# Scan heads: the second group of score matmuls issued directly behind the first, ahead of the value rows' first tile

## The chip, the cores and the metric

One Trainium2 chip, one of its eight cores. The metric is the device time of one execution in microseconds (us). The figure of a kernel is the median of its runs, and lower is better.

## The reference: what is computed

One step of a two-layer decoder trunk over 512 prompt tokens and 8 sequences of 8 new tokens (576 columns in all), with D = 1024. Each layer is an adaLN-modulated norm, an input projection, a mixer, a gate and an output projection with a gated residual. Layer 0 mixes with HGRN2, a gated linear recurrence with 8 heads (128 key features, 256 value features), and layer 1 with dilated window attention. The change lies in layer 0 only, in the part that makes each head's score matrix:

```python
q = silu(q);  f = lb + (1 - lb) * sigmoid(f + b_f);  k = 1 - f
b = cumsum(log f)                        # within a chunk
A[t, s] = sum_c q[t, c] k[s, c] exp(b[t, c] - b[s, c])    # s <= t
o = A v + (q exp(b)) S                   # S: state carried over chunks
```

## The kernel before

Five engines run programs of their own in a fixed order written by hand, and semaphores join them. TensorE (PE) is the engine that all others serve.

**Matmuls.** A projection is done in three passes of rounded fp32 operands (`w_hi`·`h_hi`, `w_hi`·`h_lo`, `w_low`·`h_hi`). ScalarE (ACT, L412) and VectorE (DVE, L419) split each weight piece into its two parts, and PE waits for `raw_split`.

**The scan of layer 0.** `pe_step(pe, h)` runs for h = 0 to 9. Step h projects the inputs of head h and scans head g = h - 1, whose keys and queries were made one step earlier. From h = 1 to 7 both are done, so what is told of a "step" below happens seven times. In order, PE does in such a step:

1. the queries of head h (`project_T`, L446), then a mean for head h - 2, then the gates of head h (L446);
2. the scores of head g, in three groups. The decay between two positions is taken level by level (1, 2, 4, ... 64 positions), and each level is a set of small matmuls with 32-column weights and 32 columns of data. `pe_grams(pe, g, 0)` does levels 0 to 2 (60 matmuls, PSUM bank `X[:, 0]`), `pe_grams(pe, g, 1)` levels 3 to 5 (20 + 16 + 16 = 52 matmuls, bank `X[:, 1]`, L1293), and group 2 the two widest levels (L1299, bank `X[:, 2]`);
3. the value rows of head h (`project_rows`, L467), four tiles of 128 tokens with 24 matmuls of 256 columns each. `project_rows` calls `between(tile)` behind each tile, and `between` puts other work there: behind tile 1 a transpose of adaLN rows (L525), score group 2 and a part of the second layer's adaLN projection (L493);
4. behind tile 3 the transposes of the scanned head's keys (`pe_turn_keys`, L1309 and L1319), which also wait for `ada_done`, that is for DVE's reading of the adaLN rows (`read_ada_chunk`, L565 and L557); in steps 1 to 6 two more adaLN projections (L493); then the sequences' rows (L1335, L1339), the chunk states (L1352), which wait for ACT's `kr` (L1013) and DVE's `kz` (L1167), and the rest. In step 7 the adaLN projections are absent, behind tile 1 as well as behind tile 3.

Meanwhile DVE reads score group 0 (L1069, L1073), makes the running sum `b_` (L1180), reads score group 1 (L1073 again), and then works through the levels of head h (L1103, L1104, L935, L936), with group 2 (L1083 to L1089), the adaLN rows and `kz` among them.

In the trace each of these score matmuls leaves two records, so that 60 are 120 records and 52 are 104.

Of the kernel before, what the change touches and what calls it, by code (L numbers as in the profile page):

```python
# [128 lines left out]
def program(nc, I, O):  # L129
    with ExitStack() as ctx:  # L130
# [133 lines left out]
        def ticket_w(h, t):  # L264
            return TICKETS * h + t
# [134 lines left out]
        def parts_of(key):  # L400
            nk, width = stream[index[key]][2:4]
            return [w[:, 0:nk * width].rearrange("p (k c) -> p k c", k=nk) for w in (hi_buffer(key), lo_buffer(key))]
# [23 lines left out]
        def begin(t):  # L426
            if t >= 2:
                wait_read(nc.tensor, t - 2)
            return t % 2
# [7 lines left out]
        def project_T(t, key, ks=range(KD), cut=HT):  # L437

            nc.tensor.wait_ge(raw_split, split_no[key][0] + 1)
            s = begin(t) if 0 in ks else t % 2  # L440
            wh, wl = parts_of(key)
            for k in ks:
                for i, (a, b) in enumerate(((wh, h_hi), (wh, h_lo), (wl, h_hi))):
                    for e in range(2):
                        n0, n1 = (0, cut) if e == 0 else (cut, T)
                        last = nc.tensor.matmul(PJ[:, 2 * s + e, 0:n1 - n0], a[:, k, :], b[:, k, n0:n1],  # L446
                                                start=(k == 0 and i == 0), stop=(k == KD - 1 and i == 2))
            if KD - 1 in ks:
                last.then_inc(pj_ready, 1)

        def row_passes(tile, k, wh, wl):

            rows = slice(tile * P, tile * P + P)
            if tile == CH:
                return ((h_hi[:, k, rows], wh), (h_hi[:, k, rows], wl))
            return ((h_hi[:, k, rows], wh), (h_lo[:, k, rows], wh), (h_hi[:, k, rows], wl))

        def project_rows(t, keys, tiles, out_of, between=None):

            begin(t)  # L460
            for tile in tiles:
                for k in range(KD):
                    if k % 4 == 0:
                        nc.tensor.wait_ge(raw_split, split_no[keys[k // 4]][0] + 1)
                    passes = row_passes(tile, k, *parts_of(keys[k // 4]))
                    for i, (a, b) in enumerate(passes):
                        last = nc.tensor.matmul(out_of(tile), a, b[:, k % 4, :], start=(k == 0 and i == 0),  # L467
                                                stop=(k == KD - 1 and i == len(passes) - 1))
                if tile == tiles[-1]:
                    last.then_inc(pj_ready, 1)  # L470
                if between:
                    between(tile)
# [830 lines left out]
        def pe_turn_keys(pe, g):  # L1303

            pe.wait_ge(lv_done, XS * g + XS)
            if g:
                pe.wait_ge(fin_done, 2 * g)
            for c in range(CH):
                pe.transpose(X[:, 3, c * P:(c + 1) * P], kh[:, c * P:(c + 1) * P], ident[:])  # L1309
            pe_turn_seq_keys(pe, g)  # L1310
# [44 lines left out]
        def pe_seq_out(pe, g):  # L1355

            pe.wait_ge(orow_done, g + 1)
            for j in range(2):
                last = pe.transpose(X[:, 2, 256 + j * P:256 + (j + 1) * P], orow[:, j * P:(j + 1) * P], ident[:])
            last.then_inc(os_ready, 1)  # L1360
# [9 lines left out]
        def pe_mean(pe, f):  # L1370

            halved = f < AH - 2
            if halved:
                pe.wait_ge(sum_done, f + 1)
            else:
                pe.wait_ge(sq_done, f + 1)
            pe.wait_ge(ub_read, f + 1)
            for bank, a, z in ((0, 0, TP), (1, TP, T)):
                for j in range(1 if halved else 2):
                    last = pe.matmul(X[:, bank, 0:z - a], ones[:], sq0[:, j, a:z], start=(j == 0), stop=(halved or j == 1))  # L1380
            last.then_inc(ms_ready, 1)

        def pe_step(pe, h):
            b, g, f = h % 2, h - 1, h - 2
            new, scan, end = h < AH, 0 <= g < AH, 0 <= f
            if new and h:
                project_T(ticket_w(h, 0), ("w", h, 0))
            if end and new:
                pe_mean(pe, f)
            if h == AH:  # L1390
                out0_units(2)
                pe_mean(pe, f)
                out0_units(3)
                pe_grams(pe, g, 0)
                out0_units(4)
                pe_grams(pe, g, 1)
                out0_units(5)
                pe_grams(pe, g, 2)
                pe_turn_keys(pe, g)
                out0_units(6)  # L1400
                pe_chunk_states(pe, g)
                pe_seq_rows(pe, g)
                out0_units(7)
                pe_seq_out(pe, g)
                out0_units(8)
            if h > AH:
                out0_units(12)
                pe_mean(pe, f)
                out0_units(14)
                pe.wait_ge(ada_done, 3 + AH)  # L1410
                pe_out(pe, "out0", 1, range(8))
            if new and h:
                project_T(ticket_w(h, 1), ("w", h, 1))
            def grams(n):
                if scan:
                    pe_grams(pe, g, n)

            keys = [("w", h, 2), ("w", h, 3)]
            if new:

                def between(tile):
                    if tile == 0:
                        grams(1)
                    if tile == 1:
                        if scan:
                            if g:
                                pe.wait_ge(fin_done, 2 * g)
                            turn_ada_groups(3 + h)
                        grams(2)
                        wait_read(pe, ticket_w(h, 1))  # L1430
                        if h < AH - 1:
                            project_ada(16 + 4 * h, 3)
                            project_ada(17 + 4 * h, 3)

                grams(0)
                project_rows(ticket_w(h, 2), keys, range(CH),
                             lambda c: PJ[:, c // 2, c % 2 * ADV:(c % 2 + 1) * ADV], between)
            if scan and new:
                pe.wait_ge(ada_done, 4 + h)
                pe_turn_keys(pe, g)  # L1440
            if new and h < AH - 1:
                project_ada(18 + 4 * h, 3)
                project_ada(19 + 4 * h, 3)
            if scan and new:
                pe_seq_rows(pe, g)
                if h < AH - 1:
                    pe_chunk_states(pe, g)
                    pe_seq_out(pe, g)
            if new:
                project_rows(ticket_w(h, 3), keys, [CH], lambda c: PJ[:, 2, 0:ADV])  # L1450
                if h == AH - 1:
                    pe_chunk_states(pe, g)
                    pe_seq_out(pe, g)
                project_T(ticket_w(h, 4), ("w", h, 4))
            if scan:
                pe.wait_ge(os_done, g + 1)
                pe.wait_ge(up_read, g + 1)
                pe.wait_ge(kz_done, g + 1)
                pe_new_states(pe, g)
            if new:  # L1460
                if h < AH - 1:
                    pe.wait_ge(adr_done, 5 + h)
                project_T(ticket_w(h, 5), ("w", h, 5), range(KD))
            elif scan:
                out0_units(10)
            if scan:
                pe.wait_ge(ua_read, g + 1)
                if h == AH:
                    pe.wait_ge(at_done, 3)
                for j in range(2):  # L1470
                    for c in range(CH):
                        out = X[:, 2 + j, c * P:(c + 1) * P]
                        last = pe.matmul(out, v_[:, g % 2, c, j * P:(j + 1) * P], at[:, c], start=True, stop=(c == 0))  # L1473
                        if c:
                            last = pe.matmul(out, sc[:, c - 1, j * P:(j + 1) * P], qe[:, g % 2, c * P:(c + 1) * P],  # L1475
                                             start=False, stop=True)
                last.then_inc(op_ready, 1)
# [51 lines left out]
        def out0_units(upto):  # L1529

            pe_out(nc.tensor, "out0", 0, range(out0_done[0], upto))
            out0_done[0] = max(out0_done[0], upto)
# [1422 lines left out]
```

## Time and profile before

| what | value |
|---|---|
| median of 3 runs | 1080.66 us (1079.57 to 1081.3) |
| the profiled execution's own time | 1077.29 us |
| its span (first to last instruction) | 1075.5 us |
| PE, PE weight loads, DVE, ACT, POOL busy | 99%, 91%, 60%, 47%, 14% of the span |
| scan steps 1 to 7 | from 95.3 to 465.2 us of the span |

The span is 1.8 us shorter than its execution's time and 5.2 us shorter than the median. PE's busy share counts the time in which at least one matmul is under way. Matmuls are pipelined, so a start-to-start distance says more about their cost than their duration does.

### The profile page before, as it was taken

Reading aid. Unit: us, or ns where it says so; the run is one execution under the profiler, and the core shown is the slowest. Engines: PE = TensorE matmul, PEld = TensorE weight load, DVE = VectorE, ACT = ScalarE, POOL = GpSimd, SP = SyncE. Lnnn points to the kernel's source line nnn. Section 1 sums busy time; section 2 is a strip of 40 time slices with the busy share of each in tenths; the row PEclk is TensorE's granted clock in tenths of the full one; section 3 lists DMA queues with packets and bytes.
Section 4 is the critical chain, followed back from the end, with each engine's and each line's share of the span. In section 5 each row is a group of like instructions: output and inputs, shape, how many; then the busy total and the mean of one; then the engine's idle time right before and its main releaser. Section 6 shows DMA issues by size and latency. Waiting matters only on the chain.

```text
span 1075.5 us, 24573 instructions
## 1 busy us (share of the span) xinstructions
PE 1059.6 (99%) x10237; PEld 974.8 (91%) x10237; DVE 644.4 (60%) x1301; ACT 507.7 (47%) x1049; POOL 145.4 (14%) x167
## 2 busy tenths in 40 slices
PE   8999999999999999999999999999999999999998
PEld 5799999999999999989998789888988998899997
DVE  3785767676868685976446754644464446447333
ACT  4653444445454545464224555545455465467122
POOL 2000010100000000000000460243025203410000
PEclk9999999999999999999999999999999999999999
DMA  9862535363536364027534464426443544543432
GB/s 320 307 200 83 176 101 177 103 177 105 177 104 177 105 177 143 26 92 249 154 88 157 112 150 128 133 62 159 129 127 91 132 134 118 113 110 102 138 103 59
DMA packets 233300, 147.80 MB, mean 137 GB/s; under 512 B 8899, under 2 KB 227229, under 8 KB 232678
## 3 DMA queue, kind: packets, MB, share of 16 engines
q1 hardware_dynamic: 218544, 134.35, 43.6%
q10 hardware_dynamic: 14646, 11.89, 3.3%
q8 instruction: 81, 1.33, 0.5%
q14 instruction: 29, 0.24, 0.1%
HBM read 124.19 MB, written 22.02 MB: 136 GB/s over the span
## 4 chain that ended last, share of the span: by engine, by line
PE 93%; DVE 3%; ACT 2%; DMA 1%; issue 0%; SPq 0%; ACTq 0%; DVEq 0%
PE PJ L446 28%; PE PJ L1805 17%; PE PJ L1495 17%; PE PJ L467 9%; PE PJ L1864 2%; PE X L1293 2%; PE X L1352 1%; PE X L1954 1%; PE X L1473 1%; PE PJ L754 1%; DMA pre<-in_ada_w_dram 1%; PE PJ L493 1%; PE X L1920 1%; PE X L1475 1%; PE X L1366 1%; PE X L1380 1%
## 5 line engine op out<-in xcount | busy, mean ns | idle before, releaser
L446 PE MATMUL PJ<-h_hi,w_hi 128*128 128x288 f32 (+2 forms) x672 | 147.4, 301 | 0.6 <-ACT v_ L1009 0.6
L446 PE MATMUL PJ<-h_lo,w_hi 128*128 128x288 f32 (+2 forms) x672 | 143.8, 295 | 0.0
L446 PE MATMUL PJ<-h_hi,w_low 128*128 128x288 f32 x672 | 139.8, 296 | 0.0
L446 PEld LDWEIGHTS PJ<-h_hi,w_hi 128*128 128x128 f32 x672 | 108.1, 189 | 3.3 <-issue 3.1
L446 PEld LDWEIGHTS PJ<-h_lo,w_hi 128*128 128x128 f32 x672 | 108.5, 189 | 0.0
L412 ACT ACTIVATE w_hi<-raw 128x1024 fp32r<-128x1024 f32 (+1 forms) x91 | 92.8, 1035 | 31.5 <-PE PJ L1805 16.1
L446 PEld LDWEIGHTS PJ<-h_hi,w_low 128*128 128x128 f32 x672 | 106.5, 189 | 0.0
L467 PE MATMUL PJ<-w_hi,h_hi 128*128 128x256 f32 x320 | 91.1, 292 | 0.8 <-DVE q_ L1129 0.8
L419 DVE TENSOR_TENSOR w_low<-raw,w_hi 128x1024 fp32r<-128x1024 f32 x64 | 77.3, 1224 | 23.7 <-ACT w_hi L412 23.3
L467 PE MATMUL PJ<-w_low,h_hi 128*128 128x256 f32 x320 | 88.1, 283 | 0.0
L1495 PE MATMUL PJ<-oz_low,w_hi 128*128 128x256 f32 (+1 forms) x400 | 85.8, 296 | 0.0
L1805 PE MATMUL PJ<-w_hi,h_hi 128*128 128x512 f32 x210 | 84.6, 403 | 0.6 <-DVE w_low L419 0.6
L963 ACT ACTIVATE dd<-dd 128x576 f32<-128x576 f32 (+1 forms) x64 | 42.1, 658 | 65.7 <-DVE dd L1104 58.1
L467 PE MATMUL PJ<-w_hi,h_lo 128*128 128x256 f32 x256 | 72.4, 283 | 0.0
L1495 PEld LDWEIGHTS PJ<-oz_low,w_hi 128*128 128x128 f32 x400 | 67.5, 190 | 0.0
L1805 PE MATMUL PJ<-w_hi,h_lo 128*128 128x512 f32 x168 | 65.7, 391 | 0.0
L467 PEld LDWEIGHTS PJ<-w_hi,h_hi 128*128 128x128 f32 x320 | 61.1, 191 | 3.7 <-issue 2.0
L1261 DVE SCALAR_TENSOR_TENSOR xT<-PJ,ada,xT 128x128 f32<-128x128 f32 (+1 forms) x40 | 17.7, 498 | 73.7 <-PE PJ L1495 70.2
L467 PEld LDWEIGHTS PJ<-w_low,h_hi 128*128 128x128 f32 x320 | 61.2, 191 | 0.0
L1785 POOL TENSOR_TENSOR ra<-rb,tsin 128x256 f32<-128x256 f32 (+1 forms) x40 | 41.5, 1056 | 92.9 <-DVE rb L1753 92.2
L1495 PE MATMUL PJ<-h_hi,w_hi 128*128 128x256 f32 x240 | 52.8, 301 | 0.0
L1795 POOL TENSOR_TENSOR rows<-rows,ra 128x512 f32<-128x512 f32 (+3 forms) x40 | 48.3, 1208 | 21.8 <-DVE rows L1768 19.0
(388 smaller groups left out, 2447.6 us busy)
## 6 DMA issues: line engine op xcount, KB each, us to landing
raw<-in_a_w_in_dram SPq DMA_DIRECT2D x48, 512.0 KB, 4.8
raw<-in_ada_w_dram SPq DMA_DIRECT2D x28, 512.0 KB, 3.9
kvc<-in_cache_kv_w_dram SPq DMA_DIRECT2D x24, 512.0 KB, 5.3
pre<-in_ada_w_dram SPq DMA_DIRECT2D x16, 512.0 KB, 9.9
s<-in_state_hgrn_dram SPq DMA_DIRECT2D x8, 1024.0 KB, 8.1
out_hgrn_sample_dram<-s ACTq DMA_DIRECT2D x8, 1024.0 KB, 5.3
raw<-in_a_w_out_dram SPq DMA_DIRECT2D x16, 512.0 KB, 4.6
raw<-in_b_w_in_dram SPq DMA_DIRECT2D x64, 128.0 KB, 2.3
```

Of the source, the lines that this page charges most:

```text
L412: act.activation(hi_buffer(key)[:, 0:size], raw_buffer(key)[:, 0:size], ACT.Copy).then_inc(hi_done, 1)
L419: dve.tensor_tensor(lo_buffer(key)[:, 0:size], raw_buffer(key)[:, 0:size], hi_buffer(key)[:, 0:size].bitcast(F32), ALU.subtract).then_inc( ...
L446: last = nc.tensor.matmul(PJ[:, 2 * s + e, 0:n1 - n0], a[:, k, :], b[:, k, n0:n1], start=(k == 0 and i == 0), stop=(k == KD - 1 and i == 2))
L467: last = nc.tensor.matmul(out_of(tile), a, b[:, k % 4, :], start=(k == 0 and i == 0), stop=(k == KD - 1 and i == len(passes) - 1))
L963: act.activation(dd[:, x % 2, 0:n], dd[:, x % 2, 0:n], ACT.Exp).then_inc(exp_done, 1)
L1261: dve.scalar_tensor_tensor(out=x, in0=y, scalar=gate, in1=x, op0=ALU.mult, op1=ALU.add)
L1293: last = pe.matmul(gram_at(i)[BL * q:BL * q + BL, n], left[:, t:t + BL], right[:, t:t + BL], start=True, stop=True)
L1495: last = pe.matmul(PJ[:, 2 * (t % 2) + e, 0:z - x], a[:, n % nk, :], b[:, x:z], start=(n == 0 and i == 0), stop=(n == 2 * nk - 1 and i == 2))
L1785: ins = nc.gpsimd.tensor_tensor(dst[:, :, :, h], src[:, :, :, 1 - h], tab.unsqueeze(1).to_broadcast([p, 2, 2, BHD // 2]), ALU.mult)
L1795: nc.gpsimd.tensor_tensor(out, out, turned, ALU.add).then_inc(rows_done, 1)
L1805: last = pe.matmul(unit_tile(j, u, c), a, b[:, k, :], start=(p == 0 and k == 0 and i == 0), stop=(p == 3 and k == 1 and i == len(passes) - 1))
L1864: last = pe.matmul(unit_tile(0, 0, c), a, b[:, k % 2, :], start=(k == 0 and i == 0), stop=(k == KD - 1 and i == len(passes) - 1))
```

## The change

The call for score group 1 leaves `between` (where it stood behind tile 0) and stands directly behind the call for group 0. Nothing else is changed: the same instructions are issued, with the same operands and waits.

```diff
             if new:
 
                 def between(tile):
-                    if tile == 0:
-                        grams(1)
                     if tile == 1:
                         if scan:
                             if g:
...
                 grams(0)
+                grams(1)
                 project_rows(ticket_w(h, 2), keys, range(CH),
                              lambda c: PJ[:, c // 2, c % 2 * ADV:(c % 2 + 1) * ADV], between)
```

The next rows are PE's, step 1, at the end of score group 0, in the kernel before. L1293 is a score matmul, L467 one of the value rows; the names in brackets are the semaphores waited for.

```order
L1293 MATMUL X<-q_,k_ 32x32 x19
L1293 MATMUL X<-qk 32x32 [waits lv_done]
L1293 MATMUL X<-qk 32x32 x19
L1293 MATMUL X<-qk 32x32 [waits lv_done]
L1293 MATMUL X<-qk 32x32 x19
L467 MATMUL PJ<-w_hi,h_hi 128x256 [waits raw_split,pj_read0]
```

The same place of the changed kernel:

```order
L1293 MATMUL X<-q_,k_ 32x32 x19
L1293 MATMUL X<-qk 32x32 [waits lv_done]
L1293 MATMUL X<-qk 32x32 x19
L1293 MATMUL X<-qk 32x32 [waits lv_done]
L1293 MATMUL X<-qk 32x32 x19
L1293 MATMUL X<-qk 32x32 [waits lv_done]
L1293 MATMUL X<-qk 32x32 x19
L1293 MATMUL X<-qk 32x32 [waits lv_done]
L1293 MATMUL X<-qk 32x32 x15
L1293 MATMUL X<-qk 32x32 [waits lv_done]
L1293 MATMUL X<-qk 32x32 x15
L467 MATMUL PJ<-w_hi,h_hi 128x256 [waits raw_split,pj_read0]
```

Three more levels (20, 16 and 16 matmuls) now stand between group 0 and the first value row. The second place is PE's, step 1, at the end of the value rows' tile 0, before:

```order
L467 MATMUL PJ<-w_hi,h_lo 128x256
L467 MATMUL PJ<-w_low,h_hi 128x256
L1293 MATMUL X<-qk 32x32 [waits lv_done]
L1293 MATMUL X<-qk 32x32 x19
L1293 MATMUL X<-qk 32x32 [waits lv_done]
L1293 MATMUL X<-qk 32x32 x15
L1293 MATMUL X<-qk 32x32 [waits lv_done]
L1293 MATMUL X<-qk 32x32 x15
L467 MATMUL PJ<-w_hi,h_hi 128x256 [waits raw_split]
L467 MATMUL PJ<-w_hi,h_lo 128x256
```

The same place of the changed kernel:

```order
L467 MATMUL PJ<-w_hi,h_hi 128x256
L467 MATMUL PJ<-w_hi,h_lo 128x256
L467 MATMUL PJ<-w_low,h_hi 128x256
L467 MATMUL PJ<-w_hi,h_hi 128x256 [waits raw_split]
L467 MATMUL PJ<-w_hi,h_lo 128x256
```

Tile 1 now follows tile 0 with nothing between them. DVE, ACT, POOL and the DMA queues issue what they did, in the order in which they did.

## Rows read from the trace of the kernel before

**Rows 1.** The page: span, then busy time, share and instructions of each engine.
```profile
span 1075.5 us, 24573 instructions
PE 1059.6 (99%) x10237; PEld 974.8 (91%) x10237; DVE 644.4 (60%) x1301; ACT 507.7 (47%) x1049; POOL 145.4 (14%) x167
```

**Rows 2.** Busy time of each engine and granted clock (PEclk), over the scan steps.
```profile
93.00:470.00 377.00, 376.66 (x5113) 354.59 (x5114) 274.03 (x601) 181.77 (x245) 24.67 (x20) 1.00 0.45 134
```

**Rows 3.** Timeline of PE, step 1: start, us taken, instruction, number of records.
```profile
95.71 0.85 PE L1293 MATMUL X<-qk 128*32 128x32 f32 x78
96.48 0.39 PE L467 MATMUL PJ<-w_hi,h_hi 128*128 128x256 f32 x1
96.71 0.28 PE L467 MATMUL PJ<-w_hi,h_lo 128*128 128x256 f32 x1
...
99.34 0.28 PE L467 MATMUL PJ<-w_low,h_hi 128*128 128x256 f32 x1
99.55 1.10 PE L1293 MATMUL X<-qk 128*32 128x32 f32 x104
100.58 0.39 PE L467 MATMUL PJ<-w_hi,h_hi 128*128 128x256 f32 x1
100.80 0.28 PE L467 MATMUL PJ<-w_hi,h_lo 128*128 128x256 f32 x1
...
103.44 0.29 PE L467 MATMUL PJ<-w_low,h_hi 128*128 128x256 f32 x1
```

**Rows 4.** The same timeline, tiles 2 and 3, which nothing parts (48 records).
```profile
105.78 0.39 PE L467 MATMUL PJ<-w_hi,h_hi 128*128 128x256 f32 x1
...
108.51 0.28 PE L467 MATMUL PJ<-w_hi,h_lo 128*128 128x256 f32 x1
108.63 0.28 PE L467 MATMUL PJ<-w_low,h_hi 128*128 128x256 f32 x1
...
111.51 0.29 PE L467 MATMUL PJ<-w_low,h_hi 128*128 128x256 f32 x1
```

**Rows 5.** Score matmuls by line: duration ns min/median/max.
```profile
L1293 PE MATMUL X<-qk x1472: 196/196/217, 95.7 to 468.3; 128*32 128x32 f32 x184
```

**Rows 6.** The same timeline as rows 3, step 2.
```profile
153.66 0.28 PE L467 MATMUL PJ<-w_low,h_hi 128*128 128x256 f32 x1
...
155.12 0.28 PE L467 MATMUL PJ<-w_hi,h_lo 128*128 128x256 f32 x1
```

**Rows 7.** Timeline of all engines, step 3, where PE's next waits lie.
```profile
219.29 0.20 DVE L557 TENSOR_TENSOR ada<-adsum,params 128x36 f32<-128x36 f32 x1
220.17 0.36 PEld L1309 LDWEIGHTS X<-ident,kh 128*128 128x128 f32 x3
221.63 0.59 ACT L1013 ACTIVATE kr<-X 128x512 f32<-128x512 f32 x1
222.27 0.42 DVE L1167 TENSOR_TENSOR kz<-X,seqm 128x256 f32<-128x256 f32 x1
223.20 0.19 PEld L1352 LDWEIGHTS X<-v_,kr 128*128 128x128 f32 x1 [0.41 <-issue]
```

**Rows 8.** The same view, step 7 (in brackets: idle before, and what ended it).
```profile
436.55 0.28 PE L467 MATMUL PJ<-w_low,h_hi 128*128 128x256 f32 x1
436.56 0.20 DVE L557 TENSOR_TENSOR ada<-adsum,params 128x36 f32<-128x36 f32 x1
436.81 0.31 PEld L1309 LDWEIGHTS X<-ident,kh 128*128 128x128 f32 x3 [0.18 <-DVE ada L557]
```

**Rows 9.** Timeline of PE and DVE, step 3: the end of score group 1 and its reading.
```profile
209.22 0.39 PE L467 MATMUL PJ<-w_hi,h_hi 128*128 128x256 f32 x1
...
209.09 1.36 DVE L1180 TENSOR_TENSOR_SCAN b_<-reset,fg 128x576 f32<-128x576 f32 x1
210.48 1.02 DVE L1073 COPY_PREDICATED atd<-lev,X 128x160 f32<-128x160 uint8 x3
```

**Rows 10.** Timeline of PE, step 1: score group 2.
```profile
104.09 0.83 PE L1299 MATMUL X<-qk 128*32 128x32 f32 x30
```

## The prediction

> **What bounds the kernel now.** I read the page first. PE has a matmul under way in 99% of the span, and the next engine, DVE, is busy in 60% of it [rows 1]. Over the scan steps PE is short of the full time by 0.34 us in 377, at a granted clock of 1.00 [rows 2]. So nothing that makes DVE or ACT earlier can give back more than that 0.34 us there. What can change the time is how long PE's own stream takes, and whether a wait appears in it that isn't there now. Busy time can't show the first, since matmuls overlap. The timeline can: the reader should look at the starts, and at what happens where one kind of matmul follows another. The chain of waits shows PE all but free of them in this stretch, so for the second I looked at how long before each of PE's waits its releaser ends.
>
> **What the moved block takes where it stands.** In step 1, tile 0's last value matmul starts at 99.34, the 104 records of score group 1 at 99.55, tile 1's first matmul at 100.58 and its second at 100.80 [rows 3]. Inside a run of value matmuls the starts are 0.12 us apart (108.51 to 108.63) [rows 4]. Here it is 0.21 us to the first score matmul, and 0.22 us from tile 1's first matmul to its second, the first of a run being the slow one each time. From 99.34 to 100.80 are 1.46 us. If tile 1 followed tile 0 directly, that stretch would be two plain distances, 0.24 us. So taking the block out frees 1.22 us. Step 2 gives the same (153.66 to 155.12) [rows 6]. A check by other rows: tiles 0 and 1 with the block between them run from 96.48 to 103.44, 6.96 us from first to last start [rows 3], and tiles 2 and 3 with nothing between them from 105.78 to 111.51, 5.73 us [rows 4]. The difference is 1.23 us.
>
> **What it takes where it goes.** Behind group 0 it joins a run of score matmuls that is already going, so it should cost its own records and no second change of kind. The run into group 0 and the run out of it to a value row exist already and stay. The rate comes from two rows. The 104 records last 1.10 us from the first start to the last end; less one duration of 0.196 us [rows 5] that is 0.90 us over 103 distances, 8.8 ns each, the run's start included. The last 78 records of group 0 last 0.85 us, so 0.65 us over 77 distances, 8.5 ns each [rows 3]. I take 8.5 ns, since the block now has no start of its own: 104 x 8.5 ns = 0.89 us. By the other rate it would be 0.91 us.
>
> Per step this gives 1.22 - 0.89 = 0.33 us of PE time (0.31 at the less favourable rate). The change thus removes one pair of changes between value and score matmuls; the arithmetic is the same. Over seven steps it would be 2.3 us.
>
> **Does PE's gain reach the end?** The value rows from tile 1 on come 0.33 us earlier, counted from the step's start, and everything behind them too, if no wait stops them. The DVE and ACT work in this part of the step hangs on the gates' projection, which ends before score group 0 and isn't moved. So each releaser keeps its place and PE moves towards it. Three waits lie behind tile 3.
>
> - `ada_done`, for the key transposes: in step 3 DVE's L557 ends at 219.49 and PE loads at 220.17 [rows 7]. Of 0.68 us, 0.35 would be left.
> - `kr_done` and `kz_done`, for the chunk states: ACT's `kr` ends at 222.22 and DVE's `kz` at 222.69, PE loads at 223.20 [rows 7]. The nearer leaves 0.51 - 0.33 = 0.18 us. A release takes about 0.05 us to act (L557 ends at 436.76, the load starts at 436.81 [rows 8]), so some 0.13 us are free. It is tight, but it holds.
> - Step 7 differs. It has no adaLN projection behind tile 1, so PE reaches the key transposes sooner than in other steps, while DVE's L557 keeps its time. The trace has PE stopped there already: tile 3's last matmul starts at 436.55, the load of the transposes at 436.81, and the idle time is put down to DVE's L557 [rows 8]. In step 3 the load starts before L557 could matter. Whatever PE gains ahead of this point in step 7 it waits off here, since L557 isn't moved. So step 7 gives nothing.
>
> What comes earlier besides: score group 1 is done some 3 us sooner. DVE reads it at 210.48, straight after the running sum that starts at 209.09 and takes 1.36 us, and the group has been done since before 209.22 [rows 9]. DVE doesn't wait for it, so it isn't helped. What comes later: tile 0, by 0.89 us. Nobody waits for tile 0 alone; the value rows are signalled as a whole behind tile 3. No queue is passed and no DMA is moved.
>
> **The sum.** Six steps x 0.33 us = 2.0 us less, step 7 nothing. The profiled execution took 1077.29 us and should take 1075.3 us; against the median of 1080.66 us it is 1078.7 us. That is 0.19% less. About 0.2%, here 2.2 us, is what a measurement of this kernel can tell from no change, so my likeliest case lies just inside "the same".
>
> **A rule against the change.** The longest runs of score matmuls now have 120 and 104 records, and the trace keeps 8.5 to 8.8 ns a record in both [rows 3]; a run of 224 is not in it. The other kind of score matmul, group 2, goes at (0.83 - 0.22)/29 = 21 ns a record [rows 10]. The Trainium skill says otherwise of short ones: in "TensorE: Matmul & The Clock Gate", section "Wait — 56ns, not 53.3ns?", start-to-start never drops below about 25 ns however few the columns. By that the added block would cost 2.6 us instead of 0.89, and each step would lose 1.4 us. The trace disagrees for these records.
>
> **The rivals.**
>
> 1. *Forecast: six steps gain, step 7 doesn't.* 1078.7 us, own range 1078.4 to 1079.0 before the noise of the runs. 60%.
> 2. *All seven gain, or a little more.* If DVE's L557 came earlier too, for instance since DVE reads group 0 while PE no longer writes scores beside it, the 2.3 us would all come, and of the 0.34 us of idle time a part: 1078.2 us. Against it: DVE's instructions there take what they take elsewhere. 10%.
> 3. *The next wait takes it in every step.* `kz_done` has 0.13 us to spare. If DVE is later by 0.2 to 0.5 us beside a denser PE, PE stops at L1352 and each step keeps 0.0 to 0.2 us: 1079.4 to 1080.7 us, say 1080.0. For it: the small margin. Against it: DVE's chain repeats within 0.1 us from step to step. 13%.
> 4. *The price isn't one of the change of kind.* If the start of a value run is slow after any long run, in proportion to that run, then joining two runs saves nothing: 1080.7 us. Against it: behind 120 records the value run's second start comes 0.23 us after its first (96.48, 96.71), behind 104 it is 0.22 us (100.58, 100.80) [rows 3]. 9%.
> 5. *Slower.* The run of 224 records outlasts what PE has in its queue, and its second half goes at the rate at which instructions come. The place is the end of group 1, the price 104 x (rate - 8.5 ns), and it decides from 1.22/104 = 11.7 ns a record. At group 2's 21 ns a step costs 2.2 instead of 1.22 us, so 1.0 us more, seven times: 1087.5 us. For it: no run here is that long. Against it: the rate doesn't fall between the 40th and the 120th record of a run. 5%.
> 6. *Something that I don't see, of either sign.* 3%.
>
> **From these to the numbers.** The predicted time is case 1's. Three runs of the kernel before lie 1.7 us apart, so the median of another few can be 0.8 us off either way. The range reaches down to case 2 less that, 1077.3, and up to case 3's 1080.0 plus half of it, 1080.4; the bounds of the rate (0.02 us a step) lie inside. Case 5's end is left out. Faster by over 0.2% needs 2.2 us: of case 1 three in ten through noise, of case 2 two in three, together with a part of case 6 27%; I say 0.32, as case 1 lies so near the line. Slower is case 5 and a part of case 6: 0.06. The rest, 0.62, is within 0.2%.
>
> **What the changed profile would show.** In each step one run of 224 score records at 8.5 ns, its second half too. No distance of 0.21 us behind tile 0, and tiles 0 and 1 in 5.73 us from first to last start. Steps 1 to 6 shorter by 0.33 us each, and step 7's idle time before L1309, 0.18 us, at about 0.5 us with the same releaser. Idle time at L1352 would speak for case 3, a rate over 9 ns in the run's second half for case 5. I am wrong if the steps shorten by the full 0.33 us and step 7 too, or if they don't shorten although the run is as described.

## The result and the profile after

The changed kernel is slower: 1092.66 us, median of four runs (1090.32 to 1094.56), beside 1080.12 us for the kernel before on the same chip (1076.83 to 1081.3, four runs). The ratio is 1.013 with a 95% interval of 1.0114 to 1.0148. The profiled executions differ by as much: 1090.32 against 1077.29 us, and 1088.5 against 1075.5 us of span, 13.0 us.

The page of the changed kernel, to set beside [rows 1], and its busy times over the scan steps, to set beside [rows 2]:

```profile
span 1088.5 us, 24573 instructions
PE 1060.7 (97%) x10237; PEld 976.8 (90%) x10237; DVE 645.8 (59%) x1301; ACT 508.0 (47%) x1049; POOL 146.0 (13%) x167
...
93.00:470.00 377.00, 366.14 (x4820) 346.56 (x4819) 267.53 (x587) 172.08 (x230) 24.21 (x20) 1.00 0.43 129
```

All engines do the work of before, in the same busy time. PE isn't slower at it, it stands still: 10.9 us of 377 without a matmul, where it was 0.34. The granted clock is still 1.00. PE's waits over the whole span, none of which the kernel before has (line, what is waited for, us in total, times, longest):

```profile
PE X L1293 <- issue: 10.5, 6, 2.3
...
PE PJ L467 <- issue: 1.4, 1, 1.4
...
PE X L1299 <- issue: 0.7, 1, 0.7
```

"issue" says that PE waited for nothing that the profile shows, so for no engine, no semaphore and no DMA of the kernel. The timeline of PE shows where. Step 1, to set beside [rows 3]:

```profile
95.13 0.53 PE L1293 MATMUL X<-q_,k_ 128*32 128x32 f32 x38
...
95.51 1.22 PE L1293 MATMUL X<-qk 128*32 128x32 f32 x121
98.54 0.73 PE L1293 MATMUL X<-qk 128*32 128x32 f32 x61 [1.80 <-issue]
99.20 0.39 PE L467 MATMUL PJ<-w_hi,h_hi 128*128 128x256 f32 x1
...
104.93 0.29 PE L467 MATMUL PJ<-w_low,h_hi 128*128 128x256 f32 x1
```

The run goes at its rate up to its 163rd record (38 + 4 + 121), then no start follows for 2.0 us, then the last 61 come at the old rate. The value rows are as predicted: tiles 0 and 1 lie 5.73 us apart from first to last start (99.20 to 104.93). The same run in steps 2 to 8:

```profile
151.52 1.64 PE L1293 MATMUL X<-qk 128*32 128x32 f32 x170
155.50 0.32 PE L1293 MATMUL X<-qk 128*32 128x32 f32 x12 [2.34 <-issue]
...
209.55 2.00 PE L1293 MATMUL X<-qk 128*32 128x32 f32 x182
211.48 0.39 PE L467 MATMUL PJ<-w_hi,h_hi 128*128 128x256 f32 x1
...
267.20 0.60 PE L1293 MATMUL X<-qk 128*32 128x32 f32 x44 [2.02 <-issue]
...
322.06 0.27 PE L467 MATMUL PJ<-w_low,h_hi 128*128 128x256 f32 x1
323.75 0.28 PE L467 MATMUL PJ<-w_hi,h_hi 128*128 128x256 f32 x1 [1.41 <-issue]
...
377.81 0.86 PE L1293 MATMUL X<-qk 128*32 128x32 f32 x76 [1.12 <-issue]
...
434.54 0.45 PE L1293 MATMUL X<-qk 128*32 128x32 f32 x28 [2.12 <-issue]
...
479.66 1.09 PE L1293 MATMUL X<-qk 128*32 128x32 f32 x104 [1.13 <-issue]
```

Read from the end of the run (224 records, three value matmuls more in step 5), the standstills lie behind record 163, 212, 180, 227, 148 and 196 of steps 1, 2, 4, 5, 6 and 7. Step 3 has only 0.25 us from one start to the next, behind record 132. The place moves from step to step, though each of them but the last issues the same. So it belongs not to the step but to something that counts through.

**What counts through.** These windows of the whole kernel end in the standstills of steps 1, 2, 4, 5, 6 and 7; in brackets behind PE and PEld are the matmuls and weight loads in each.

```profile
0.00:97.50 97.50, 90.68 (x852) 78.90 (x853) 57.82 (x121) 50.78 (x66) 7.59 (x13) 1.00 0.75 243
97.50:154.00 56.50, 54.62 (x760) 51.73 (x759) 39.62 (x86) 26.12 (x35) 3.70 (x3) 1.00 0.45 134
154.00:266.00 112.00, 109.62 (x1390) 103.85 (x1390) 77.97 (x171) 50.94 (x69) 7.48 (x6) 0.98 0.45 135
266.00:322.90 56.90, 55.14 (x758) 52.24 (x759) 39.86 (x87) 26.15 (x35) 3.71 (x3) 1.00 0.44 133
322.90:377.20 54.30, 52.95 (x632) 50.09 (x631) 37.87 (x85) 24.50 (x34) 3.71 (x3) 1.00 0.47 139
377.20:433.50 56.30, 54.62 (x759) 51.73 (x759) 40.08 (x86) 26.62 (x35) 3.33 (x3) 1.00 0.52 153
```

From one standstill to the next PE issues 1519, 2780, 1517, 1263 and 1518 matmuls and loads, and the trace has 17 to 19 semaphore instructions of PE in each such stretch (36 in the double one). With these the sums are 1536, 2816, 1536, 1280 and 1536, each a multiple of 256. The DMA view has a queue that answers to it, here over the whole span, over 96 to 97 us and, as a row of the windows, over 97 to 98 us:

```profile
q8 instruction: 81, 1.33, 0.5%
...
q8 instruction: 1, 0.02, 5.8%
...
97.00:98.00 1.00, 0.00 (x0) 0.00 (x0) 1.00 (x1) 1.00 (x1) 0.00 (x0) 1.00 0.00 0
```

PE has 2 x 10237 matmuls and loads and 345 semaphore instructions, 20819 in all, and the 81 packets carry 257 each. So a packet of instructions holds 256. One was under way in step 1's run for 0.93 us (5.8% of 16 engines in 1 us), from 96.15 to about 97.1. In the next microsecond no DMA was at work, DVE and ACT ran, and PE stood. The Trainium skill names the same unit: in "Runtime: NRT & Kernel Launch", section "Instruction fetch mechanics", PE's instruction memory is filled in blocks of 256, the next one while the current one runs. The trace agrees. The Trainium skill also says there that the cost of crossing into a block is mostly hidden. Over the scan steps of the kernel before the trace agrees (no wait of PE for "issue"), in the joined runs it doesn't (10.9 us).

**Theory.** PE gets its instructions in packets of 256. The transfer of the next packet starts near the moment at which PE passes into the one it is working on, and PE can go on some 2.2 to 3.0 us after that transfer's start. The passing lies 128 score matmul records and their loads ahead of each standstill (in step 1 at record 35 of the run, 95.43). For the changed kernel, from the times of q8's packets in the trace:

| step | PE passes at record | q8's transfer starts, us after that | PE goes on, us after the transfer's start |
|---|---|---|---|
| 1 | 35 | 0.71 | 2.39 |
| 2 | 84 | 0.94 | 2.71 |
| 3 | 4 | -1.17 | 2.52 |
| 4 | 52 | 0.98 | 2.35 |
| 5 | 99 | 0.98 | 2.25 |
| 6 | 20 | 0.06 | 2.36 |
| 7 | 68 | 1.09 | 2.33 |

A stretch of 256 instructions with few score matmuls lasts long enough to hide this. One made of them alone is 128 records and their loads, lasts 1.1 us at 8.5 ns, and PE stands at its end for what is left: it goes on 3.10 to 3.65 us after the passing in steps 1, 2, 4, 5 and 7. In step 6 it is 2.4 us, and in step 3, whose packet was under way before the run began, 1.4 us. The row of that packet, from the DMA view over 208.0 to 209.1 us (the run starts at 209.17):

```profile
q8 instruction: 1, 0.02, 6.4%
```

So two things set the length of a standstill: how fast the 256 instructions are used up, and how soon their successor's transfer starts. It starts sooner where the passing lies near the run's start (records 4 and 20 in the table). That the supply runs some instructions ahead of the matmuls, which is long in time while long matmuls are at work, would give this; no run shows it by itself. The expectations below reckon with 3.1 to 3.6 us from the passing throughout. Where the end of a packet falls in a step depends on the number of instructions since the program's start. **Rivals.** *Run length:* PE or its queue can hold only so many score matmuls in a row, and the place varies for another reason. *Clock:* the power throttle stops PE in dense stretches. *The new neighbour:* something in DVE's or ACT's work beside group 1 does it.

**Where the 13.0 us are.** From the start of one score run to the next, steps 1 to 7 took six times 54.32 and then 43.99 us before. After they took 56.01, 58.03, 54.25, 56.25, 55.56, 55.31 and 45.79 us, 11.3 us more. The standstills are 12.1 us. Another 1.5 us come behind that of step 2, where PE runs at half its clock (1.2 in place of 2.4 GHz) for 3.4 us: the starts of value matmuls are 0.21 us apart there, not 0.12.

```profile
156.56 0.41 PE L467 MATMUL PJ<-w_hi,h_hi 128*128 128x256 f32 x1
156.77 0.42 PE L467 MATMUL PJ<-w_hi,h_lo 128*128 128x256 f32 x1
...
157.00:159.00 2.00, 2.00 (x11) 2.00 (x11) 1.86 (x5) 0.68 (x1) 0.00 (x0) 0.50 0.24 70
```

Against that stand the predicted gain, 6 x 0.33 = 2.0 us, and 0.5 us in step 7, which leaves 11.1 of the 11.3 us. Of the span's 13.0 us another 1.9 arise from step 8 on, where both kernels issue the same and the changed one stands still at 479.66 and at L1299; ahead of step 1 the changed kernel is 0.2 us earlier.

### The profile page after: what moved, and what is told of

It reads as the page before. It is cut to its first block, busy times and chain, and to the rows that moved or that the text cites. A ratio compares the mean times of both kernels' runs of the same rounds, so it can differ in the third digit from the quotient of the medians.

```text
span 1088.5 us, 24573 instructions
## 1 busy us (share of the span) xinstructions
PE 1060.7 (97%) x10237; PEld 976.8 (90%) x10237; DVE 645.8 (59%) x1301; ACT 508.0 (47%) x1049; POOL 146.0 (13%) x167
## 4 chain that ended last, share of the span: by engine, by line
PE 92%; DVE 3%; issue 2%; ACT 1%; SPq 1%; DMA 1%; ACTq 0%; DVEq 0%
PE PJ L446 27%; PE PJ L1804 17%; PE PJ L1494 16%; PE PJ L467 9%; PE PJ L1863 2%; PE X L1293 2%; PE X L1352 1%; PE X L1953 1%; PE X L1472 1%; PE PJ L754 1%; PE PJ L493 1%; PE X L1919 1%; PE X L1474 1%; DMA pre<-in_ada_w_dram 1%; SPq L2704 1%
## 5 line engine op out<-in xcount | busy, mean ns | idle before, releaser
L467 PE MATMUL PJ<-w_hi,h_hi 128*128 128x256 f32 x320 | 91.2, 293 | 2.2 <-issue 1.4
L467 PE MATMUL PJ<-w_low,h_hi 128*128 128x256 f32 x320 | 88.7, 285 | 0.0
L467 PE MATMUL PJ<-w_hi,h_lo 128*128 128x256 f32 x256 | 73.1, 285 | 0.0
L467 PEld LDWEIGHTS PJ<-w_hi,h_hi 128*128 128x128 f32 x320 | 61.9, 193 | 3.4 <-issue 2.0
L467 PEld LDWEIGHTS PJ<-w_low,h_hi 128*128 128x128 f32 x320 | 62.0, 194 | 0.0
```

## The experiments

"After" is the changed kernel, "before" the other. A pad is a 32x32 fp32 matmul of ones into a corner of `X` that is written anew before it is read. Like a score matmul it leaves two records and two weight loads, so it is four instructions. "Record 163" is the 163rd of a run of 224.

**1. Shift the count.** After, and at the program's start:

```diff
+            for _ in range(32):
+                pe.matmul(X[0:BL, 0, 0:BL], ones[:, 0:BL], ones[:, 0:BL], start=True, stop=True)
             first_pe(pe)
```

> The changed kernel with 32 more 32x32 fp32 matmuls of the ones tile ahead of the first transposes, where PE idles for 0.6 us: 128 more PE instructions, half of a 16 KB instruction packet of 256, and about 0.55 us of PE work. They leave the results alone. In the changed kernel's trace PE stands still in the 224-record score run of steps 1, 2, 4, 5, 6, 7 and not of step 3, after 163, 212, 180, 224, 148 and 196 records, each time at the same place modulo 256 of PE's own instruction count. Theory F (instruction fetch: PE has one packet of 256 instructions of runway, the next is asked for when the last is begun and is there some 3.3 us later, while the score run uses up a packet in 1.1 us): all places move by 64 records, so step 3 now stalls, after about 199 records and for about 2.3 us, and step 7 doesn't; the stalls stand at about records 227 (in the value rows), 148, 199, 244, 160 and 212 of steps 1, 2, 3, 4, 5, 6. Total within 3 us of the changed kernel's, 1088 to 1094 us. Rival Q (a queue that empties in any run of more than some 130 records, wherever it stands): the same steps stall at the same records as in the changed kernel. Rival C (TensorE's clock falls in a long run of small matmuls): stalls of 2 us without a change of granted clock aren't explained, and the places stay.

Measured: 1092.80 us (one run). The standstills of steps 1 to 8 lie behind records 227, 148, 196, 243, 164, 212, 132 and 190, within four records of what was expected. That of step 4 lasts only 0.3 us. Steps 3, 6 and 7 (of 224 records the last 28, the last 12, and none behind a standstill over 0.3 us):

```profile
211.94 0.62 PE L1293 MATMUL X<-qk 128*32 128x32 f32 x28 [2.10 <-issue]
...
382.24 0.32 PE L1293 MATMUL X<-qk 128*32 128x32 f32 x12 [2.33 <-issue]
...
436.30 2.01 PE L1293 MATMUL X<-qk 128*32 128x32 f32 x182
```

Step 3, which had been spared, now stands for 2.1 us, and step 7 is spared and takes 43.99 us. The scan's instructions are the same. That fells the new neighbour. The clock as a cause falls by the rows of the changed kernel: the granted clock is 1.00 in the microsecond in which PE has no matmul (97 to 98), and the one stretch at half clock among the steps (156.56 to 159.97) begins after the standstill of step 2 has ended.

**2 to 4. A step of a whole number of packets.** 24 pads a step bring its instructions from 1440 to 1536, six packets, so that the place can't move; the number of pads at the start picks the place.

```diff
+            for _ in range(14):     # 39 in the second kernel
+                pe.matmul(X[0:BL, 0, 0:BL], ones[:, 0:BL], ones[:, 0:BL], start=True, stop=True)
...
             nc.tensor.wait_ge(ada_done, c)
+            for _ in range(24):
+                nc.tensor.matmul(X[0:BL, 3, 0:BL], ones[:, 0:BL], ones[:, 0:BL], start=True, stop=True)
```

> The changed kernel with 24 more 32x32 fp32 matmuls of the ones tile (48 records, 96 instructions) in each of steps 1 to 7, ahead of the adaLN transposes behind tile 1, so that a step has 1536 instructions, six packets, in place of 1440; and 14 more in the prologue, so that the packet boundary stands at about record 7 of the score run in every step, as it does in step 3 of the changed kernel. Work is added, none is left out. Theory F: no stall in any score run, although each still has 224 records; 7 x 0.41 us of added matmuls and about 2.0 us gained by the joined runs (step 7 waits for DVE): 1079 to 1083 us, about 10 us faster than the changed kernel. Rival Q: all steps stall as in the changed kernel, and with the added work it is 1094 to 1097 us.

> As the kernel before this one in the list, with 39 matmuls in place of 14 in the prologue: the packet boundary stands at about record 85 of the score run in all seven steps, as in step 2 of the changed kernel, which had the longest stall (2.54 us). The two kernels differ by 25 small matmuls ahead of the first transposes (0.4 us). Theory F: every step stalls for 2.2 to 2.6 us, after about 213 records: 7 x 2.4 = 17 us more than the other, 1096 to 1101 us, and more if the clock falls behind a stall. Rival Q: the same time as the other, within 1 us.

> The kernel before with the same added matmuls as the second kernel of this list (24 in each of steps 1 to 7, 14 in the prologue): the control for their cost. Both theories: no stall, 7 x 0.41 = 2.9 us and at most 0.2 us of prologue more than the kernel before, 1082.5 to 1084 us. The difference from the second kernel is what the joined runs are worth when nothing stalls: by the prediction's arithmetic 6 x 0.33 = 2.0 us in favour of the joined ones, with step 7 giving nothing since PE waits there for DVE's reading of the adaLN rows. If the added matmuls use up that wait in step 7, 2.3 us.

Measured: 1091.29 us with 14 pads (four runs, ratio 1.012, 1.0103 to 1.0137), 1116.62 us with 39 (one run), and 1091.27 us for before with 14 (four runs, 1.0121, 1.01 to 1.0141). All three are outside what was expected. A pad in one 32-column part of the array takes 32 ns a record, not 8.5, so that the pads cost 1.77 us a step (56.09 in place of 54.32) where I had put 0.41. The difference between the first two, 25.3 us where I had put 17 and more with a lower clock, holds the pads on both sides, so the pair still tells what it was made for. The last of the 224 records, steps 1 and 2 with 39 pads, and the wait row of that kernel over the scan steps:

```profile
101.44 0.32 PE L1295 MATMUL X<-qk 128*32 128x32 f32 x11 [2.40 <-issue]
...
161.29 0.42 PE L1295 MATMUL X<-qk 128*32 128x32 f32 x10 [2.34 <-issue]
...
PE X L1295 <- issue: 16.1, 7, 2.4
```

All seven runs stand behind record 213 or 214, for 2.2 to 2.6 us, and behind six of them PE is at half its clock for 3.4 us, so that a step takes 59.7 to 59.9 us. With 14 pads one run passes whole (step 5), three stand for 0.2 us (2, 4, 7) and three for 0.5 to 0.9 us. There PE passes at record 7 or 8 and the transfer had started 0.5 to 1.4 us before; with 39 it starts 0.9 to 1.1 us behind the passing. The run is equally long in both kernels, and 25 small matmuls (100 instructions) at the start make 25 us. That fells run length.

**5 and 6. The boundary at record 124, and its control.** After and before, both with 20 pads at the start and 24 a step.

> As e2_lock_free, with 20 matmuls in the prologue in place of 14: the packet boundary stands at record 124 of the score run in every step, so that the next one falls 27 matmuls into the value rows, some 3.5 us behind the first. In e2 some steps still stalled for 0.2 to 0.9 us (the boundary at record 8). Theory F, with 3.1 to 3.6 us from a boundary to the next packet's arrival: no stall at all in steps 1 to 7, each score run 2.05 us long as in step 5 of e2. Rival Q (any run over 130 records stalls): stalls as in the changed kernel. Against its control, the next kernel, 6 x 0.32 = 1.9 us less, in step 7 nothing or up to 0.3 us (the added matmuls may use up the wait for DVE): 1.9 to 2.2 us less by the prediction's own arithmetic. Absolute: 1088 to 1091 us, the added matmuls being 1.8 us a step (measured in e4_before_pads).

> The control of e5_joined_124: the kernel before with the same added matmuls, score groups apart. Both theories: no stall in steps 1 to 7, every step 56.09 us as in e4_before_pads, 1090 to 1092 us.

Measured: 1092.36 us (four runs, ratio 1.0133, 1.0107 to 1.0158) and 1094.53 us (four runs, 1.0149, 1.0129 to 1.017), both above the expected 1088 to 1091 and 1090 to 1092 us. PE's waits over the scan steps of the fifth kernel have no row. Steps 1 and 2, and the same run in step 5:

```profile
96.54 1.74 PE L1295 MATMUL X<-qk 128*32 128x32 f32 x182
98.21 0.39 PE L467 MATMUL PJ<-w_hi,h_hi 128*128 128x256 f32 x1
...
152.32 1.74 PE L1295 MATMUL X<-qk 128*32 128x32 f32 x182
153.99 0.39 PE L467 MATMUL PJ<-w_hi,h_hi 128*128 128x256 f32 x1
...
319.79 1.95 PE L1295 MATMUL X<-qk 128*32 128x32 f32 x182
```

From the run's start (96.16 and 151.94) 2.05 us each to the first value row: 224 records at their old rate, to the last. In steps 4, 5 and 7 the start behind record 124 comes 0.1 to 0.2 us late (1.95 in place of 1.74 us in step 5), too little for a row of the waits. The expectation left this boundary out: it lies only 1.8 us behind the one before, and by a fixed 3.1 to 3.6 us PE would have stood for over 1.3 us in every step. The transfer had started 0.3 to 2.3 us before the passing. Over steps 1 to 7 the joined order took 380.39 us and the other 382.11, 1.7 us less: six steps with 0.11 to 0.32 us each (55.77 to 55.98 against 56.09) and 0.20 us in step 7. The steps that gain least, 4 and 5, are two of the three with a late start. The medians are 2.2 us apart, but the control comes 2.0 us later to step 1, with 6.8 us at half clock ahead of it, so I go by the steps.

**7. Half of tile 0 between the groups.** Before, with group 1 behind the first 12 of tile 0's 24 value matmuls.

```diff
+                if between and tile == 0 and k == 3:
+                    between(-1)
...
-                    if tile == 0:
+                    if tile == -1:
                         grams(1)
```

> The kernel before with score group 1 behind the first 12 of tile 0's 24 value matmuls in place of all 24; same instructions, same number of changes between kinds, other distance. Theory F: a boundary at record 35 to 85 of group 0 is followed by the next after 1.1 us of score matmuls and 1.8 us of value matmuls and changes, 2.9 us in all, against the 3.1 to 3.6 us that a packet needs: stalls of 0.2 to 0.7 us in steps 1, 2, 4, 5, 7, nothing or 0.2 us in steps 3 and 6; 1 to 4 us slower than before with up to 2.4 us from step 8 among them: 1079.5 to 1083 us. Rival Q (the length of an unbroken score run decides, here 120 and 104 as before): no stall, the time of before, 1078.5 us.

Measured: 1083.32 us (one run, 0.3 us above the expected range). Five standstills of 0.6 to 0.9 us, behind records 163, 211, 179, 227 and 195 of the score records and value matmuls together, none in steps 3 and 6. The wait row over the scan steps, and that of step 2 in the timeline:

```profile
PE X L1295 <- issue: 2.5, 5, 0.7
...
154.59 0.40 PE L1295 MATMUL X<-qk 128*32 128x32 f32 x25 [0.52 <-issue]
```

Set beside the changed kernel's standstills at the same counts, twelve value matmuls (1.44 us) take 1.1 to 1.8 us off each, and there is no unbroken run of 224 here.

**8. Only level 3 joined.** Runs of 160 and 64 records, tile 0 between them.

```diff
                 grams(0)
+                grams(1, slice(0, 1))
...
                     if tile == 0:
-                        grams(1)
+                        grams(1, slice(1, 3))
```

> The kernel before with the first level of group 1 (20 matmuls, 40 records) joined to group 0 and the other two levels left behind tile 0: runs of 160 and 64 records. Theory F: a stall only where the boundary behind group 0's own falls inside or just behind the run of 160: step 1 (boundary at record 35, the next 3 matmuls into the value rows) 1.4 to 2.0 us, step 6 (records 20 and 148) 1.3 to 1.6 us, step 3 up to 0.3 us, step 4 up to 0.3 us, none in steps 2, 5, 7: 3 to 4 us and up to 2.4 us from step 8, 1081 to 1085 us. Rival Q (runs over some 130 records stall): all seven steps stall alike.

Measured: 1081.24 us (one run). Standstills behind records 163 (1.4 us), 132 (0.3), 179 (0.3) and 148 (1.5) of steps 1, 3, 4 and 6, none in 2, 5, 7 and 8. Step 1, behind the third value matmul, step 6, and step 2 without one:

```profile
99.13 0.39 PE L467 MATMUL PJ<-w_hi,h_hi 128*128 128x256 f32 x1 [1.14 <-issue]
...
151.96 1.21 PE L1294 MATMUL X<-qk 128*32 128x32 f32 x118
...
156.15 0.76 PE L1294 MATMUL X<-qk 128*32 128x32 f32 x64
...
372.13 0.32 PE L1294 MATMUL X<-qk 128*32 128x32 f32 x12 [1.35 <-issue]
```

**9 and 10. Small matmuls by themselves.** Before, and ahead of group 0 of step 0, where nothing else is changed, 256 small matmuls in a row.

```diff
+                    for i in range(256):
+                        q = BL * (i % 4)     # 0 in the second kernel
+                        pe.matmul(X[q:q + BL, 1, 0:BL], ones[:, 0:BL], ones[:, 0:BL], start=True, stop=True)
```

> The disputed cost by itself: the kernel before with 256 small 32x32 fp32 matmuls of the ones tile (512 records, 1024 instructions, four packets) ahead of the value rows of step 0, where nothing is scanned. They go over the four 32-column parts of the array in turn, as the score matmuls do, at some 8.5 ns a record. They read and write nothing that the kernel uses, and a whole number of packets leaves the later boundaries where they are. By the count of instructions the boundaries fall at records 23, 151, 279 and 407 of the run. Theory F: one stall at each of the last three, of 1.3 to 2.5 us, 128 records apart; none behind the run; steps 1 to 7 as in the kernel before, 54.32 us. Run 512 x 8.6 ns = 4.4 us and 5 to 7 us of stalls. Rival Q (something that fills or empties with the number of small matmuls, a queue or a PSUM port): a stall once at the start or a slower rate all through, not three at multiples of 128 records.

> As e9_long_fast with the same count of instructions, but all 256 matmuls write the same 32 rows of the array's output. So they go at 32 ns a record, as the added matmuls of e4_before_pads did: 512 x 32 ns = 16.4 us. Theory F: a packet of 128 records now lasts 4.1 us, longer than the 3.1 to 3.6 us that the next one needs, so there is no stall at any of the four boundaries, though the run is the longest of all. Rival Q: stalls as in e9_long_fast, or more.

Measured: 1089.94 and 1094.75 us (one run each). With the four 32-column parts in turn:

```profile
52.36 1.48 PE L1438 MATMUL X<-ones 128*32 128x32 f32 x151
56.38 1.54 PE L1438 MATMUL X<-ones 128*32 128x32 f32 x128 [2.54 <-issue]
60.93 1.93 PE L1438 MATMUL X<-ones 128*32 128x32 f32 x128 [3.01 <-issue]
64.38 1.62 PE L1438 MATMUL X<-ones 128*32 128x32 f32 x105 [1.52 <-issue]
```

The 256 matmuls are 512 records. The standstills take 1.8 to 3.3 us from start to start, where I expected up to 2.5; the second and third fall into 10.2 us at half clock. PE stands behind record 151, 279 and 407, 128 records and their 128 loads apart, and the steps behind it are 54.32 us as before. The packets' transfers start 1.5, 2.3 and 1.1 us behind the passings, and PE goes on 2.2 to 2.3 us after each. In one part only, at 32 ns a record:

```profile
53.02 9.02 PE L1437 MATMUL X<-ones 128*32 128x32 f32 x279
63.10 7.54 PE L1437 MATMUL X<-ones 128*32 128x32 f32 x233 [1.06 <-issue]
...
59.00:61.00 2.00, 2.00 (x69) 2.00 (x67) 1.97 (x5) 0.94 (x2) 0.00 (x0) 1.00 0.74 215
```

One standstill is left where I expected none. The instruction packets of that stretch start at 55.29, 60.62, 64.22 and 67.97, so the second came 5.3 us behind the first, and 2.8 us behind PE's passing, at a time when the DMA engines were busy for 74 to 82%. Over the scan steps that share is 43 to 45%. PE went on 2.5 us after that start, as elsewhere: late was the start, not the transfer (1.0 us). That the other transfers delay it is a possible reading; no run varied them.

**11 and 12. A few instructions more or less.** Before with 11 of its 12 warm-up matmuls, and after with two pads at the start.

> The kernel before with 11 in place of 12 warm-up matmuls at its very start, 4 PE instructions fewer; they leave the results alone. In step 8 the scores' two groups stand 6 matmuls apart in all kernels. The changed kernel lost 1.9 us more there, by stalls at records 126 of the score run and 254 (1.44 and 0.94 us), and the kernel before none, with the same count of instructions: by count the packet boundary lies 1 to 2 records ahead of the run's start, right at the wait that opens it. Theory F, with the addition that PE's front end passes the boundary early only if it isn't held by that wait: two records later the boundary is behind the wait, so step 8 now stalls at records 128 and 256, for 0.8 to 1.7 us each, and steps 1 to 7 don't: 1.5 to 2.5 us slower than before. If the addition is wrong: no stall, the time of before.

> The changed kernel with 2 more small matmuls in the prologue, 8 PE instructions more: each boundary falls 4 records sooner. Steps 1, 2, 4, 5, 6, 7 stall as in the changed kernel, 4 records sooner (after 159, 208, 176, 223 or the start of the value rows, 144, 192 records), step 3 not or by 0.2 us. In step 8 the boundary is now 5 records ahead of the run and its wait; with the addition of the experiment before, step 8 doesn't stall and the time is 1.5 to 2.5 us less than the changed kernel's but for its clock; without it, as the changed kernel's: 1088 to 1093 us.

Measured: 1081.41 and 1095.87 us (one run each; 1.1 us above the kernel before where 1.5 to 2.5 was expected, and above the expected 1088 to 1093 us). In the first, steps 1 to 7 are as before, and step 8 stands twice; its row for the first of them:

```profile
468.83 1.07 PE L1293 MATMUL X<-qk 128*32 128x32 f32 x102 [1.47 <-issue]
```

In the second every standstill of steps 1 to 7 comes four records sooner (159, 208, 128, 176, 224, 144, 192), as expected. Behind four of them, in steps 2, 4, 5 and 7, PE is at half clock for 3.4 us. Step 8 stands at 122 and 250 all the same. I had thought that its standstill comes or not by which side of a wait the boundary falls on; that idea is not borne out.

## Why the prediction was wrong

The step that failed is the first sentence of what the block takes where it goes: that it "joins a run of score matmuls that is already going, so it should cost its own records". The rate of 8.5 ns is right, in the run's second half too (fifth kernel). But I took a rate seen in runs of 120 and 104 records as one that PE can hold. It holds only while its instructions are there, and tile 0 (24 value matmuls, 2.9 us for 48 instructions) was what gave the next packet its time: in steps 1 to 7 of the kernel before, 256 instructions of which score matmuls are a part last 4.0 us or more, but for one stretch of 2.6 us in step 3, whose packet's transfer had started 1.2 us before the passing. I had named the value rows as the place from which a change of kind is paid, not as cover. Taking them out of the run moved no instruction's own cost, and cost 12.1 us of standstills in seven steps.

- *The gain on PE.* 0.33 us a step: borne out. Step 5 stands from 322.06 to 323.75, 1.57 us more than the usual 0.12; its 55.56 us less that are 53.99, and 54.32 less 0.33 is 53.99. Fifth against sixth kernel it is 0.32 us in the best step and 0.25 us on the mean of the six; where it is less, part of it goes to the late start at record 124 (0.20 us in step 5).
- *Step 7.* I had it give nothing. The fifth kernel gains 0.20 us in it. This doesn't test the forecast: the pads use up the wait for L557 that it rests on (they cost the control 1.58 us in step 7, 1.77 in the others). In the changed kernel the wait for L557 is gone, because PE comes late, and the step lost 1.80 us with a standstill of 2.3: the wait's 0.18 us and the freed 0.33 us were both taken off it. The size was small either way. So rival 2 isn't decided either.
- *Rival 3, `kz_done`.* Not seen, and hardly tested: neither the changed kernel nor the fifth has a wait at L1352 or L1309, but PE comes later to them in both, by the standstills or by the pads. In no step without pads is PE ahead of the kernel before by more than 0.16 us (step 4 of the first kernel, 54.16 us). So that the freed 0.33 us would pass these waits, as the forecast has it, stays unshown.
- *Rival 4, the price isn't of the change of kind.* Fallen with the gain.
- *Rival 5, slower.* Right in its ground, the supply of instructions, and in its sign. Wrong in its form: no slower rate from some record on, but full rate and then 1.3 to 2.5 us of nothing (0.25 in step 3), at a place that moves by step and can be record 148 or the value rows behind the run. Its price of 7 us was about half of the 12.5 us measured. I gave it 5% because "the rate doesn't fall between the 40th and the 120th record", which could say nothing about it: the trace of before shows no standstill in a run of 120 because the value rows around it make its packet last longer.
- *The floor on starts.* The Trainium skill's 25 ns between starts ("TensorE: Matmul & The Clock Gate", section "Wait — 56ns, not 53.3ns?") would also have said slower. By the prediction's own working that is 1.4 us a step. The trace of the changed kernel goes on at 8.5 ns (224 records in 2.05 us), so it had the sign by another cause.

Open is what sets the start of a packet's transfer. It covers the two things left: why PE goes on 3.1 us after a passing in one place and 1.4 or over 5 in another, and why the scores of step 8 stand still in the changed kernel and in most of the experiments, and not in before, 8 and 9. In those three the transfer starts 1.9 to 2.5 us ahead of step 8's run, in the changed kernel, 7, 11 and 12 it starts 0.6 to 0.9 us behind the run's start. No version beats the kernel before: the joined run is worth 2 us at most, and the filling that lets it pass costs 1.8 us a step here.

## What to carry to other kernels

Count PE's instructions, not only its time. Where 256 instructions in a row (here 128 matmul records with their loads, or 64 fp32 matmuls of the code) take less than some 3.6 us, PE can stand still at their end for up to the difference, and a few long matmuls among the short ones help; even half a tile took 1.1 to 1.8 us off each standstill. It need not: where the transfer had started ahead of the passing, 256 instructions in 1.1 to 3.0 us passed with nothing or with up to 0.9 us of standstill (kernels 2, 4 and 5). When PE is idle for "issue", look at the instruction queue in the DMA view and at the count of instructions since the last such place before looking at semaphores.

## What the runs showed of the hardware that was not expected

- In every standstill of steps 1 to 7 and of the ninth and tenth kernels PE went on 2.2 to 3.0 us after the start of its instruction packet's transfer, of which the transfer itself is 0.9 to 1.4 us. In the changed kernel 1.5 us passed between its end (97.08) and PE's next start (98.54), with no DMA at work. The transfer's start lay between 1.4 us ahead of PE's passing into the packet before (second kernel) and 2.8 us behind it (tenth).
- The place of a standstill can be set to within four records by small matmuls at the program's start, 400 us earlier (kernels 1 and 12). So an edit anywhere ahead can move such a kernel by microseconds.
- A standstill of over 2 us can be followed by 3.4 us at half clock, which costs 1.3 to 1.5 us more. It did so behind one of the seven standstills of steps 1 to 7 in the changed kernel's profile and behind six of seven in the third kernel. In the eleventh it came behind one of 1.5 us.
- Small matmuls that stay in one 32-column part of the array start 32 ns apart, those that go round the four parts 8.5 ns.
